# Neighbourhood attention beside an S5 mixer on one core: values loaded, weights streamed, branches summed in PSUM

## The reference, cut to what matters

```python
o = gates[...,0:1]*softmax(q kc^T) vc + gates[...,1:2]*softmax(q ks^T) vs + gates[...,2:3]*softmax(q kw^T) vw
y = s5_mixer(zs);  y = y * sigmoid(y @ w_glu + b_glu)
mix = concat(rmsnorm(o, attn_norm_g), rmsnorm(y, ssm_norm_g))     # each 512 wide
x = x + gt1 * (mix @ w_o)
```

## Time and profile before

| | before |
|---|---|
| median of 3 runs | 2847.0 us (2841.59 to 2849.22) |
| the profiled execution's own time | 2846.76 us |
| its span | 2844.9 us |
| mean granted TensorE clock | 0.946 |
| PE busy | 2700.9 us, 95% of the span |
| attention, first scores to last values | 219.8 us |
| last scores to the end of the w2o products | 99.3 us |

### The profile page before, as it was taken

One profiled execution on the slowest core, in us unless ns is written; L12 is line 12 of the kernel. 1 busy time (PEld: TensorE's weight loads), 2 busy tenths in 40 slices (PEclk: granted clock), 3 DMA queues, 4 the chain that ended last, 5 costly groups with the idle time before them and its releaser, 6 DMA issues.

```text
span 2844.9 us, 33286 instructions
## 1 busy us (share of the span) xinstructions
PE 2700.9 (95%) x13744; PEld 2222.7 (78%) x13744; DVE 1504.0 (53%) x2308; ACT 995.7 (35%) x1480; POOL 405.3 (14%) x410
## 2 busy tenths in 40 slices
PE   7999999999999989999999999999799997999998
PEld 3888888879888878966888778888588874588786
DVE  4765445367777777177522555544535332443444
ACT  4212121246556553134422332323323333343343
POOL 0101000114544451000000010100001000020110
PEclk8999999999999999999999999999996568999999
DMA  7444445323111122020322233333124211222221
GB/s 293 156 178 178 181 179 194 128 75 112 63 53 64 48 81 84 16 89 1 118 90 91 110 102 125 117 136 132 69 76 126 66 37 67 93 90 101 99 84 43
DMA packets 58248, 294.60 MB, mean 104 GB/s; under 512 B 14705, under 2 KB 19953, under 8 KB 30193
## 3 DMA queue, kind: packets, MB, share of 16 engines
q1 hardware_dynamic: 56944, 282.52, 27.4%
q10 hardware_dynamic: 1152, 9.96, 0.9%
HBM read 271.75 MB, written 20.71 MB: 103 GB/s over the span
## 4 chain that ended last, share of the span: by engine, by line
PE 83%; DVE 9%; ACT 6%; issue 1%; DMA 0%; POOL 0%; DVEq 0%; SPq 0%; POOLq 0%; ACTq 0%
PE ps L314 81%; DVE wl L929 1%; PE ps L3138 1%; DVE hd L1575 1%; ACT x L1530 1%; ACT wh L920 0%; DVE x L1609 0%; DMA x<-in_x 0%; ACT hd L1514 0%; ACT hd L1512 0%; DVE hd L1577 0%; ACT L678 0%; DVE at L1627 0%; ACT L1512 0%; DVE dd L1653 0%
## 5 line engine op out<-in xcount | busy, mean ns | idle before, releaser
L314 PE MATMUL ps<-xs,wh 128*128 128x512 f32 (+1 forms) x2816 | 785.6, 366 | 17.7 <-DVE xs L963 13.6
L314 PEld LDWEIGHTS ps<-xs,wh 128*128 128x128 f32 x2816 | 509.3, 190 | 104.8 <-issue 16.5
L314 PE MATMUL ps<-xs,wl 128*128 128x512 f32 (+1 forms) x1408 | 513.4, 365 | 0.0
L314 PE MATMUL ps<-h,wh 128*128 128x512 f32 (+1 forms) x1408 | 391.0, 364 | 8.3 <-POOL h L1162 8.3
L913 DVE TENSOR_TENSOR wl<-w,wh 128x2048 fp32r<-128x2048 f32 (+4 forms) x114 | 244.1, 2143 | 254.7 <-ACT wh L907 254.5
L907 ACT ACTIVATE wh<-w 128x2048 fp32r<-128x2048 f32 (+4 forms) x114 | 204.4, 1794 | 321.8 <-PE ps L314 274.3
L314 PEld LDWEIGHTS ps<-xs,wl 128*128 128x128 f32 x1408 | 267.6, 190 | 42.6
L314 PEld LDWEIGHTS ps<-h,wh 128*128 128x128 f32 x1408 | 253.5, 189 | 51.7 <-POOL h L1162 10.0
L314 PE MATMUL ps<-x1h,wh 128*128 128x512 f32 x584 | 240.6, 412 | 26.3 <-DVE at L1627 17.0
L314 PE MATMUL ps<-h,wl 128*128 128x512 f32 (+1 forms) x704 | 255.9, 363 | 0.0
L314 PE MATMUL ps<-x1h,wl 128*128 128x512 f32 x584 | 235.6, 403 | 0.0
(11 more groups left out here) (461 smaller groups left out, 4504.6 us busy)
## 6 DMA issues: line engine op xcount, KB each, us to landing
w<-in_adat SPq DMA_DIRECT2D x52, 1024.0 KB, 5.0
w<-in_f1i SPq DMA_DIRECT2D x22, 1024.0 KB, 6.6
w<-in_f2i SPq DMA_DIRECT2D x22, 1024.0 KB, 4.9
w<-in_f3i SPq DMA_DIRECT2D x22, 1024.0 KB, 4.8
s_tables<-t ACTq DMA_DIRECT2D x4, 2368.0 KB, 8.5
w<-in_ada SPq DMA_DIRECT2D x8, 1024.0 KB, 8.9
w<-in_whf SPq DMA_DIRECT2D x8, 1024.0 KB, 4.8
w<-in_whqg SPq DMA_DIRECT2D x8, 1024.0 KB, 4.7
```

The costliest lines, as they stand in the source:

```text
L314: return e.matmul(out, l, r, start=st, stop=sp)
```

## The change

**Weights are scaled before they are turned.** A new item `weights` follows each unit by one step: DVE forms the unit's reciprocal and multiplies it with the gate (two operations on 128 x 2), POOL multiplies both branches' weights in `PB` with it (two operations, 128 x W, in place), and PE's turn waits for POOL. In exchange `combine` no longer scales or adds.

**Values are loaded, weights stream.** `turned` comes two steps after its unit, its squares are written so that two heads lie side by side, and `values` runs once for two heads: 64 columns of values are loaded and 256 columns of weights stream, for both branches, all summed in one bank, of which each pair has half. The compressed branch is a further product of that sum (31 rows, 256 columns). Its weights are scaled by DVE before they are turned, and its fourth piece is gone. The result is by features already; `combine` is now two copies by DVE (64 partitions x 256) per four units straight into `mix`, which is not normed.

**The norm by features, at the end.** `normed` is gone. `act_glu`, `dve_glu` and `pe_glu` take squares, their sum, Ln and Exp of `mix`'s lower half ("an"), and `dve_norm` scales it. The w2o products of output tiles 0 to 3 first run with the lower half ("an"), then with the upper ("ss"), and tiles 4 to 7 run both halves in turn.

Buffers move: `PB` is now `RP`, `PT` is two of 2048 columns, S5's `YT` is `TB`.

```diff
-        out = [("comp", 0, s) for s in range(4)]
-        for n in range(34):
+        out = [("comp", 0, s) for s in range(3)]
+        for n in range(36):
             out += s5_step(n, S5V)
             if n < 32:
                 out.append(("scores", n))
-            if n >= 2:
-                out.append(("values", n - 2))
+            if 2 <= n < 34:
+                out.append(("turned", n - 2))
+            if n >= 4 and n % 2 == 0:
+                out.append(("values", (n - 4) // 2))
             if n < 32:
                 out.append(("maxima", n))
-            if n >= 2 and n % 4 == 1:
-                out.append(("combine", n - 2))
             if 1 <= n < 33:
-                out.append(("turned", n - 1))
+                out.append(("weights", n - 1))
+            if n >= 6 and n % 4 == 2:
+                out.append(("combine", (n - 6) // 4))
             if n < 32:
                 out.append(("exps", n))
-            if n >= 9 and (n - 10) % 8 == 0 and n >= 10:
-                out.append(("normed", (n - 10) // 8, 1))
...
# pool_att
+            elif item == "weights":
+                i, h, W = AU[n]
+                w.wait_ge(*ivV.at(n, "gate"))
+                for y in range(2):
+                    p = PB[(2 * n + y) % 4][:, 0:W]
+                    e.tensor_tensor(p, p, RS[(n // 4) % 2][:, y, h % 4:h % 4 + 1].to_broadcast([128, W]),
+                                    ALU.mult).then_inc(*wtG.of(n, y))
# dve_att
+                    tt(scv, scv, r.unsqueeze(2).to_broadcast(wide), ALU.mult).then_inc(*cmV.of(n, "scaled"))
...
+            elif item == "weights":
+                i, h, W = AU[n]
+                r, q = [z[(n // 4) % 2][:, :, h % 4:h % 4 + 1] for z in (RS, SUM)]
+                w.wait_ge(*exA.at(n, 1))
+                if n >= 8:
+                    w.wait_ge(*wtG.at(n - 8, 1))
+                e.reciprocal(r, q).then_inc(*ivV.of(n, "inv"))
+                w.wait_ge(*ivV.at(n, "inv"))
+                w.wait_ge(*vnV.at(i, "gate"))
+                tt(r, r, gv[:, i, h:h + 1, 1:3].rearrange("p h y -> p y h"), ALU.mult).then_inc(*ivV.of(n, "gate"))
             elif item == "combine":
...
+                for o in range(2):
+                    e.tensor_copy(mix[64 * o:64 * o + 64, 2 * kv:2 * kv + 2, 128 * i:128 * i + 128],
+                                  b[:, :, o, :]).then_inc(*cbV.of(n, o))
# pe_att
-                    w.wait_ge(*exA.at(n, y))
+                    w.wait_ge(*wtG.at(n, y))
                     for c in range(0, W, 128):
                         m = e.transpose(t[:, c:c + 128], p[:, c:c + 128], ident)
...
+                w.wait_ge(*cmA.at(i, "t", kv))
+                mm(e, o, VC[0:31, 64 * kv:64 * kv + 64], PCT[i % 2][0:31, 512 * kv + c.start:512 * kv + c.stop], True, False)
+                w.wait_ge(*tnA.at(2 * n + 1, 1))
                 w.wait_ge(*vnV.at(i, "cp"))
                 for y in range(2):
                     for s in range(i + 1):
-                        m = mm(e, o, pt[:, 128 * s:128 * s + 128], vn[:, s, 128 * y + 64 * kv:128 * y + 64 * kv + 64], s == 0,
-                               s == i)
+                        m = mm(e, o, vn[:, s, 128 * y + 64 * kv:128 * y + 64 * kv + 64],
+                               blocks(2 * n)[:, (i + 1) * y + s, :, :].rearrange("p h t -> p (h t)"), False, y == 1 and s == i)
# act_glu
+        w.wait_ge(*cbV.at(7, 1))
+        for m in range(4):
+            act_square(e, w, "an", mix, TL, m, SQA)
...
+        w.wait_ge(*statP.at("an"))
+        act_rsqrt(e, w, "an", banks("an"), TL, 512, W5)
# dve_glu
+        for m in range(3):
+            dve_square(e, w, "an", TL, m, SQA)
...
+        dve_norm(e, w, "an", mix, 4, vec("g_attn"), W5, mix, gnV)
# pe_glu
-        pe_squares(e, w, "ss", TL, 4, SQS)
-        w.wait_ge(*nrA.at(3, "mix", 3))
+        pe_squares(e, w, "an", TL, 4, SQA)
...
+        for m_ in range(4):
+            banks.take(w, "w2o", m_)
+            out(m_, "an")
+            if m_ == 0:
+                pe_squares(e, w, "ss", TL, 4, SQS)
+        for m_ in range(4):
+            out(m_, "ss")
+        for m_ in range(4, 8):
+            banks.take(w, "w2o", m_)
+            out(m_, "an")
+            out(m_, "ss")
         pe_squares(e, w, "n3", TL, KT, SQS)
```

More of the change, by code:

```diff
@@ L3195, in build @@
     SQS = [q8[:, k, :] for k in range(KT)]
+    SQA = SQS[4:8]
     f3_first = [("f3i", j, 2048) for j in range(2)]
@@ L3249, in pe_glu, with out @@
             banks.give(("glu", m_), (glA, "sig", m_))
-        pe_squares(e, w, "ss", TL, 4, SQS)
-        w.wait_ge(*nrA.at(3, "mix", 3))
-        for m_ in range(8):
+        pe_squares(e, w, "an", TL, 4, SQA)
+        def out(m_, norm):
             ap, there = weight(("w2o", m_ // 2, 2048))
@@ L3255, in pe_glu @@
             w.wait_ge(*there)
[L3256 removed]
             c = 128 * (m_ % 2)
[L3258 to L3263 removed]
+            b = banks("w2o", m_)
+            for k in range(4):
+                w.wait_ge(*gnV.at(norm, k))
+                kk = k + (4 if norm == "ss" else 0)
+                m = mm(e, b, wv[:, kk, c:c + 128], mix[:, kk, :], kk == 0, kk == KT - 1)
+            if norm == "ss":
+                m.then_inc(*glP.of("o", m_))
+                banks.give(("w2o", m_), (glV, "x", m_))
+        for m_ in range(4):
[9 more added lines that the diff above has]
+            out(m_, "ss")
         pe_squares(e, w, "n3", TL, KT, SQS)
```

133 lines of the change are left out of this document (29 added, 104 removed).

## The result

The changed kernel takes 2822.8 us (median of 6 runs, 2813.2 to 2834.5) against 2847.2 us before (6 runs): a ratio of 0.9912, 95% interval [0.9885, 0.994]. The profiled execution took 2822.58 us (span 2820.8). The forecast was 2808, in a range of 2782 to 2844.

A forecast was written before the change was run, and what follows sets the result against it. PE's own work was taken as the bound, with 158 of 219.8 us of attention at 1.2 GHz. The sum was 2846.8 - 2.5 - 47 + 23 - 2.7 - 9.5 = 2808 us, range 2782 to 2844.

The forecast's parts named there:

- Head: Before the first scores: PE drops 16 compressed-branch records but waits for DVE's chain; -2.5 us, between 0 and -4.
- Values at equal clock, nothing: Attention's value products: 16 records of 256 columns take 3.5 and 6.8 us against 3.68 and 6.94 before; no gain.
- the other end: New value records in attention carry the overhead of `scores`, 0.074 us each: 12 us at low clock, 6 at full.
- The clock: Attention blocks 1 to 3: 94 us of PE's low-clock time turn to full clock and shrink by half; -47 us.
- New waits: Attention, where PE is fast: turns wait for the scaling chain, in pairs and S5 rounds; +23 us, between 8 and 45.
- slowing of POOL by DVE's two-input work: POOL's weight scaling beside L3079 to L3082 in attention: some 3 us more by the worst reading, not in the sum.
- The pairs: Unit pairs in attention: the second turn waits 1.4 us per pair for POOL's scaling; 13 us over 12 pairs.
- Work moved behind the last scores: Before the last scores PE has one unit of values and one turn less to do; -2.7 us.
- the tail: From the last scores to w2o's end: GLU products at full clock, second norm hidden, end at +89.8; -9.5 us.
- Rival 4: Attention waits come as forecast but each lets the clock fall, leaving half of -47; 2831 to 2850, chance 0.12.
- Rival 3: POOL becomes attention's bound at 2.09 us per 512 columns, and longer waits hold the clock down; 2880 us, chance 0.08.
- Rival 1: Attention's clock does not follow the stream's length and no waits appear; 2832, up to 2844 us, chance 0.2.

The follow-up runs named there:

- e9: Changed kernel with the value products' sides exchanged back (128 columns of weights loaded, 64 of values streamed, compressed branch too), all else kept; 2894.1 us.
- e5: Changed kernel with each value product streaming 128 columns of one head instead of 256, so twice as many records; 2824.1 us.
- e1: Changed kernel with 128 columns of values loaded in every value product instead of 64; 2825.4 us.
- e3: Changed kernel without GpSimd's scaling of the weights, so turns wait for the exponentials alone and the output is not gated or divided; 2795.4 us.
- e7: Changed kernel with the scaling on ScalarE instead of GpSimd and each step's S5 scan items placed behind the weights; 2810.4 us.
- e6_act: Changed kernel with the scaling of the weights on ScalarE, behind its copies of the turned weights, instead of GpSimd; 2799.7 us.

## Why the prediction was right, and where its sizes were off

The time came out 15 us above the forecast and 24 below the kernel before, by the forecast's mechanism: PE at a higher clock for the same work, minus new waits, minus a shorter tail. Step by step:

1. *Head*, -2.5: measured -2.45.
2. *Values at equal clock, nothing*: right. 0.427 and 0.216 us for a record, as taken; the other end (0.074 more per record, from `scores`) did not come. At group changes 0.1 to 0.19 us come on top, some 2 us over 16 groups, which I had not counted.
3. *The clock*, -47: measured (159.6 - 103.4) / 2 = -28. This is the term that was mis-sized most, by 19 us. Of the low time I left 28 us in block 0, 26 in block 1, 10 in block 2 and none in block 3; measured were 42, 37, 17 and 7. Block 0's 6.8 us at full clock behind the turns of the compressed branch were lost, block 1 rose only at 2223, and short dips cut blocks 2 and 3. The reason I gave in the prediction, a short load and a long stream, was right in the pair and wrong in each half: e9 shows the sides to be worth 75 us of clock, but e5 halves the stream and e1 doubles the load without a change in the time. That the clock rises in every pair of blocks 2 and 3 was too simple: it was up before block 2 began and dipped four times (at 2243.8, 2254.0, 2264.3 and 2295.0).
4. *New waits*, +23: measured +13.5. For the S5 rounds I put 10 us (5 on a round in block 1 and 3 on one in block 2, which is 8 as written) and 10.1 was measured, but the agreement is luck: it is 3.3, 1.8, 2.5 and 2.6 us in four rounds, and 3.3 of it in block 0, where I had none because I took waits to vanish at low clock. I named DVE's and POOL's S5 work ahead of the weights, which is part of it, and not the data from DRAM (2.5 us of the 10.1). I also took POOL's price next to the scans as 1.264 for 512 columns and left the slowing of POOL by DVE's two-input work out of the sum, at some 3 us by its worst reading. It is there: eight scalings beside the scans took 1.31 to 1.74 us where others of their widths take 0.40 to 0.83, 7.2 us more on POOL in four rounds, 5.5 of it in the three where PE waited. The pairs were 2.3 us instead of 13: POOL took 1.04 us, not 1.264, for 512 columns, the two halves were ready 3.1 and 4.1 us after scores(O) instead of 3.5 and 4.7, which makes 0.6 us per pair in block 3, and the seven waits of pairs lie in the last two blocks (0.6 and 1.7 us), none in block 1.
5. *Work moved behind the last scores*, -2.7, and *the tail*, -9.5: the stage's difference is explained by clock and idle alone (-28.1 + 13.5 = -14.6 against -14.3), so something made up for the moved turn and values; the group changes are a part, the rest is not traced. The tail brought -7.4. The turn of the last unit but one waited 2.08 us, because DVE had two masks and two minima of the last unit ahead of its reciprocal. That wait was in the forecast (turned at +5.1, measured +5.2). What was not is the clock, which fell in the wait and stayed low for 6.8 us: the next values ended at +11.4 instead of +9.1. GLU products took 13.8 us (13.9 forecast), and w2o ended at +91.9 instead of +89.8.

The errors of steps 3 and 4 have opposite signs, which kept the sum close. They were also not independent as I had put them: e3 takes the scaling away and wins 9.6 us of idle and 18.8 by the clock. Rival 4 (each wait lets the clock fall) came nearer than the forecast, 2831 against 2822.8; its mechanism is not confirmed, since e7 has less idle and no better clock. Rival 3 is out: POOL was busy 70 of 196 us and took 1.04 us for 512 columns where it would have had to take 1.8; what it feared did happen to nine narrower scalings. Rival 1 is out by the 56 us less of low time and by e9.

The two rules that rival 1 used fare no better after the change. In e7_act_order the clock rose behind scores (2.0 us), four turns and eight turns of the compressed branch (2.9 us), with no other work in between. The Trainium skill, TensorE: Matmul & The Clock Gate, Part 4, PE-mode transpose, has it that turns do not count as work that raises the clock; the row does not bear it out, though the scores may have had a part. And e9's PE is busy in the profile for 254.7 of 260.2 us at a mean clock of 0.51, where by Part 1 of the same page of the Trainium skill a busy PE runs at full clock.

The faster version found on the way is e6_act: 2799.6 us is the median of its ten runs in two sets, which are 0.9854 [0.9827, 0.9881] and 0.9841 [0.9813, 0.9868] of the kernel before, about 25 us under the changed kernel.

## What to carry to other kernels

Ask of each product which side is loaded and which streams. With 128 columns loaded for 64 streamed, TensorE was "busy" in the profile all the time here and stood at 1.2 GHz for 253 of 260 us. With the sides exchanged, so that the stream was at least as long as the load, the work took the same time at equal clock and was done in 196 us. When a step with sums, reciprocals and a scaling is put in front of a product, look at everything that stands ahead of it in the queues of all engines of that chain, since waits that cost nothing before now reach TensorE. Look also at what runs beside it: GpSimd's scaling took 2.1 to 3.4 times as long next to VectorE's scans, ScalarE's did not. A mean over a group hides this, so read the single instructions. And bound a clock effect by its own measurement, as it did not follow from idle time here.

## What was not expected of the hardware

- The same PE records at the same distances left the clock at 1.2 GHz in one kernel and raised it to 2.4 in another.
- A kernel with 12.0 us of idle PE (e6_act) ran at a mean clock of 0.83 in the stage, one with 3.9 us at 0.73.
- With 64 columns loaded, a stream of 128 columns takes 0.213 and 0.109 us at the two clocks, half of 256 columns (0.427 and 0.216). With 128 loaded, 256 streamed take the same 0.427 and 0.216.
- GpSimd's product with a broadcast operand takes 0.40 us for 128 columns and 1.04 for 512 when nothing disturbs it, and 1.31 to 1.74 for 128 to 384 columns beside VectorE's scans; ScalarE's scaled copy between two buffers of SBUF takes 0.39 and 0.73 and is not slowed by them.
